# Feed-forward stages of a decoder trunk: two matmuls per weight tile instead of three, with the PSUM halves added at eviction

## What is computed

```python
D_MODEL, SEQ, DEPTH, D_FF = 1024, 256, 2, 2816
def swiglu(x, w_gate, w_up, w_down):
    return (jax.nn.silu(x @ w_gate) * (x @ w_up)) @ w_down
for i in range(DEPTH):
    h = h + 0.5 * swiglu(rms_norm(h, norm_ff1[i]), ffn1_gate[i], ffn1_up[i], ffn1_down[i])
    h = h + mixer_i(rms_norm(h, norm_mix[i]))
    h = h + 0.5 * swiglu(rms_norm(h, norm_ff2[i]), ffn2_gate[i], ffn2_up[i], ffn2_down[i])
return rms_norm(h, final_norm)
```

## Time and profile before

| | |
|---|---|
| median of 3 runs | 1134.71 us (1133.36 to 1139.84) |
| span of the profiled execution | 1132.6 us |
| PE busy | 1096.6 us, 97% |
| DVE busy | 752.8 us |
| ACT busy | 661.7 us |
| POOL busy | 169.1 us |
| mean DMA rate | 165 GB/s |

### The profile page before, as it was taken

How to read it: one execution, slowest core, us unless ns; L and a number is a source line. 1 busy time by engine, 2 the same in 40 slices (tenths; PEclk the granted TensorE clock), 3 DMA queues, 4 the chain that set the end, 5 groups by cost and what they waited for, 6 DMA issues and landing times.

```text
span 1132.6 us, 23053 instructions
## 1 busy us (share of the span) xinstructions
PE 1096.6 (97%) x8831; PEld 1068.1 (94%) x8831; DVE 752.8 (66%) x1028; ACT 661.7 (58%) x903; POOL 169.1 (15%) x156
## 2 busy tenths in 40 slices
PE   6999999999998999999999999999999989999996
PEld 5999999998888999999999999999988889999996
DVE  6666655799889766666546666654687677666643
ACT  5767643665876557675436676543545657676442
POOL 7000011223352420000120000012110040000011
PEclk9999999998999999999999999999999999999998
DMA  8766676444442656666765666765543336666761
GB/s 239 206 180 182 193 205 169 137 132 131 124 117 77 196 163 200 185 184 180 204 174 165 179 180 181 203 192 161 172 126 96 91 99 198 183 183 179 215 170 37
DMA packets 364307, 186.55 MB, mean 165 GB/s; under 512 B 5456, under 2 KB 363984, under 8 KB 364256
## 3 DMA queue, kind: packets, MB, share of 16 engines
q1 hardware_dynamic: 364000, 185.26, 57.7%
q0 software_dynamic: 256, 0.59, 0.2%
HBM read 184.78 MB, written 1.05 MB: 164 GB/s over the span
## 4 chain that ended last, share of the span: by engine, by line
PE 88%; DVE 7%; issue 2%; ACT 1%; POOL 1%; DMA 0%; DVEq 0%; ACTq 0%; SPq 0%; POOLq 0%
PE psum L187 27%; PE psum L188 27%; PE psum L189 27%; DVE wlo L175 1%; PE psum L1220 1%; DVE arena L868 1%; PE psum L1205 1%; POOL sumsq L270 1%; PE psum L639 1%; DVE xn L254 0%; PE psum L1219 0%; POOL sq L266 0%; DMA h<-in_xT 0%; PE psum L663 0%; DVE arena L856 0%
## 5 line engine op out<-in xcount | busy, mean ns | idle before, releaser
L187 PE MATMUL psum<-xn,whi 128*128 128x256 f32 x1888 | 543.6, 288 | 12.8 <-DVE wlo L175 12.2
L188 PE MATMUL psum<-xn,whi 128*128 128x256 f32 x1888 | 536.9, 284 | 0.0
L189 PE MATMUL psum<-xn,wlo 128*128 128x256 f32 x1888 | 536.6, 284 | 0.0
L175 DVE TENSOR_TENSOR wlo<-raw,whi 128x1024 fp32r<-128x1024 f32 (+1 forms) x317 | 419.2, 1341 | 42.4 <-ACT whi L170 41.6
L170 ACT ACTIVATE whi<-raw 128x1024 fp32r<-128x1024 f32 (+1 forms) x322 | 353.2, 1113 | 58.6 <-PE psum L189 53.2
L187 PEld LDWEIGHTS psum<-xn,whi 128*128 128x128 f32 x1888 | 364.6, 193 | 18.7 <-DVE wlo L175 10.5
L188 PEld LDWEIGHTS psum<-xn,whi 128*128 128x128 f32 x1888 | 365.2, 193 | 1.6 <-issue 1.4
L189 PEld LDWEIGHTS psum<-xn,wlo 128*128 128x128 f32 x1888 | 365.0, 193 | 0.0
L187 PE MATMUL psum<-hid,whi 128*128 128x256 f32 x896 | 254.2, 284 | 2.5 <-DVE hid L1011 1.6
L188 PE MATMUL psum<-hid,whi 128*128 128x256 f32 x896 | 253.5, 283 | 0.0
L189 PE MATMUL psum<-hid,wlo 128*128 128x256 f32 x896 | 253.5, 283 | 0.0
(11 more groups left out here) (186 smaller groups left out, 760.0 us busy)
## 6 DMA issues: line engine op xcount, KB each, us to landing
raw<-in_ffn_gate SPq DMA_DIRECT2D x88, 512.0 KB, 3.7
raw<-in_ffn_up SPq DMA_DIRECT2D x88, 512.0 KB, 4.8
raw<-in_ffn_down SPq DMA_DIRECT2D x64, 704.0 KB, 5.7
raw<-in_hyb_w_in SPq DMA_DIRECT2D x36, 512.0 KB, 3.7
raw<-in_dif_w_qkv SPq DMA_DIRECT2D x24, 512.0 KB, 4.3
raw<-in_hyb_w_out SPq DMA_DIRECT2D x16, 512.0 KB, 4.7
raw<-in_dif_w_o SPq DMA_DIRECT2D x8, 512.0 KB, 4.5
h<-in_xT SPq DMA_DIRECT2D x2, 512.0 KB, 5.4
```

The source lines that it names most:

```text
L175: dve.tensor_tensor(wlo[:, s, 0:k * P], raw[:, s, 0:k * P], whi[:, s, 0:k * P].bitcast(F32), ALU.subtract).then_inc(s_wlo, 1)
L187: pe.matmul(acc, w_hi, x[:, t, 0, :], start=start and j == 0, stop=False)
L188: pe.matmul(acc, w_hi, x[:, t, 1, :], start=False, stop=False)
L189: mm = pe.matmul(acc, w_lo, x[:, t, 0, :], start=False, stop=stop and j == k - 1)
```

## The change

For each weight tile one matmul of 512 columns multiplies `whi` with both parts of the activations, into a whole PSUM bank: the left half collects whi times the rounded part, the right half whi times the rest. A second matmul of 256 columns adds wlo times the rounded part to the right half. So a tile takes two matmuls, and a gate/up pair takes two banks; four banks hold two pairs. The output is the sum of the halves. For gate and up, ACT copies the right halves of both banks to the SBUF tile `cor` (`corrections`), DVE adds the left halves to it (`merge`, after which the banks are free), and a new DVE operation multiplies by `rb` (`normalize`). In the DVE step, the split of the gate block now stands ahead of the eviction, and the split of the up block between `normalize` and `product`. On ACT the copy stands between the two splits, and the silu behind the second. For the down products `down_out` adds the halves to `h` one after the other. The two mixers are as before.

```diff
+        def multiply_wide(pe, b, s, k, x, k0, acc, start=True, stop=True, need=None):
+            pe.wait_ge(s_wlo, b + 1)
+            for j in range(k):
...
+                pe.matmul(acc, w_hi, x[:, t, :, :], start=start and j == 0, stop=False)
+                mm = pe.matmul(acc[:, T:2 * T], w_lo, x[:, t, 0, :], start=False, stop=stop and j == k - 1)
+            mm.then_inc(s_blk, 1)
+        def wide(g, m):
+            return banks[(2 + m, m)[g]]
+        def wide_parts(g):
+            pair = psum[:, 2:4, :] if g == 0 else psum[:, 0:2, :]
+            return pair[:, :, 0:T], pair[:, :, T:2 * T]
...
+            def corrections(p, g):
+                act.wait_ge(s_blk, p * 2 + 2)
+                act.activation(cor[:, g, :, :], wide_parts(g)[1], ACT.Copy).then_inc(s_cor, 1)
...
-                act.wait_ge(s_gu, q + 1)
+                act.wait_ge(s_gn, q + 1)
                 act.activation(act_g[:, g, :], gu[:, g, 0, :], ACT.Silu).then_inc(s_silu, 1)
...
                         if m == 0:
-                            silu(it * 2 + (hb - 2 + g), g)
+                            corrections(it * 2 + (p0 - 2 + g), g)
+                    silu(it * 2 + (hb - 2 + g), g)
                     hidden_hi(it * 2 + (hb - 2 + g), g, it * 2 + (g - 2))
...
-            def scale(p, q, g, early=False):
+            def merge(p, q, g, early=False):
                 dve.wait_ge(s_blk, p * 2 + 2)
                 if not early:
                     dve.wait_ge(s_hlo, q - 1)
-                dve.tensor_tensor(gu[:, g, :, :], both(g), rb2, ALU.mult).then_inc(s_gu, 1)
+                dve.wait_ge(s_cor, q + 1)
+                dve.tensor_tensor(gu[:, g, :, :], wide_parts(g)[0], cor[:, g, :, :], ALU.add).then_inc(s_gu, 1)
+            def normalize(q, g):
+                dve.wait_ge(s_gu, q + 1)
+                dve.tensor_tensor(gu[:, g, :, :], gu[:, g, :, :], rb2, ALU.mult).then_inc(s_gn, 1)
...
-                scale(it * 2 + (p0 - 2 + g), q, g, early)
                 split_lo(dve, it * 4 + (2 * p0 + 2 * g), 2 * g, DT)
+                merge(it * 2 + (p0 - 2 + g), q, g, early)
+                normalize(q, g)
+                split_lo(dve, it * 4 + (2 * p0 + 2 * g + 1), 2 * g + 1, DT)
                 product(q, g)
-                split_lo(dve, it * 4 + (2 * p0 + 2 * g + 1), 2 * g + 1, DT)
                 hidden_lo(q, g, it * 2 + (g - 2))
...
-            add_residual(dve, n, d, half(p, 0), 0.5)
+            acc = wide(0, d % 2)
+            dve.scalar_tensor_tensor(h[:, d, :], acc[:, T:2 * T], 0.5, h[:, d, :], ALU.mult, ALU.add).then_inc(s_hr, 1)
+            dve.wait_ge(s_hr, hidden_before(n) // FT * DT + d + 1)
+            dve.scalar_tensor_tensor(h[:, d, :], acc[:, 0:T], 0.5, h[:, d, :], ALU.mult, ALU.add).then_inc(s_h, 1)
```

More of the change, by code:

```diff
@@ L127, in trunk @@
         s_gu = sem("s_gu")
+        s_cor = sem("s_cor")
+        s_gn = sem("s_gn")
         s_silu = sem("s_silu")
@@ L191, in multiply @@
                 mm.then_inc(s_blk, 1)
+        def multiply_wide(pe, b, s, k, x, k0, acc, start=True, stop=True, need=None):
+            pe.wait_ge(s_wlo, b + 1)
+            for j in range(k):
+                t = k0 + j
+                if need:
+                    need(t)
+                w_hi, w_lo = tile_of(whi, s, k)[:, j, :], tile_of(wlo, s, k)[:, j, :]
+                pe.matmul(acc, w_hi, x[:, t, :, :], start=start and j == 0, stop=False)
[6 more added lines that the diff above has]
+            return pair[:, :, 0:T], pair[:, :, T:2 * T]
         def half(pair, m):
@@ L270, in residual_square, with sums_bank @@
             pool.tensor_tensor(sumsq[:], sumsq[:], sq[:], ALU.add).then_inc(s_acc, 1)
+        def sums_bank(n):
+            wide_phase = n == len(phases) or phases[n][0] == "ffn"
+            return banks[4 if wide_phase else 2][:, 0:T]
         def token_sums(pe, n):
@@ L279, in token_sums @@
                 pe.wait_ge(s_const, 32)
-            mm = pe.matmul(SUMS, ones, sumsq[:], start=True, stop=not end)
+            mm = pe.matmul(sums_bank(n), ones, sumsq[:], start=True, stop=not end)
             if end:
                 pe.wait_ge(s_sq, (DT - 1) * (n + 1))
-                mm = pe.matmul(SUMS, ones, sq[:], start=False, stop=True)
+                mm = pe.matmul(sums_bank(n), ones, sq[:], start=False, stop=True)
             mm.then_inc(s_stat, 1)
@@ L289, in token_rms @@
                 act.wait_ge(s_rb, n)
-            act.activation(rms[:], SUMS, ACT.Sqrt, scale=1.0 / D, bias=eps[:, 0:1]).then_inc(s_rms, 1)
+            act.activation(rms[:], sums_bank(n), ACT.Sqrt, scale=1.0 / D, bias=eps[:, 0:1]).then_inc(s_rms, 1)
         def token_scale(dve, n):
@@ L332, in ffn_tensor, with gate_up @@
             p0, p1, hb = first[n], first[n] + FT, hidden_before(n)
-            def gate_up(p, g, need=None):
+            def gate_up(p, g, need=None, before_up=lambda: None):
                 for m in range(2):
-                    multiply(pe, p * 2 + m, 2 * g + m, DT, xn, 0, half(g, m), need=need if m == 0 else None)
+                    if m == 1:
+                        before_up()
+                    multiply_wide(pe, p * 2 + m, 2 * g + m, DT, xn, 0, wide(g, m), need=need if m == 0 else None)
             def down(p, g, need=None):
                 for m in range(2):
-                    multiply(pe, p * 2 + m, 2 * g + m, KD, hid, m * KD, half(g, 0), start=m == 0, stop=m == 1,
-                             need=need)
+                    multiply_wide(pe, p * 2 + m, 2 * g + m, KD, hid, m * KD, wide(0, g), start=m == 0, stop=m == 1,
+                                  need=need)
             if n:
                 read_out(pe, p0 - 2)
-            gate_up(p0, 0, lambda t: pe.wait_ge(s_xlo, DT * n + t + 1))
+            gate_up(p0, 0, lambda t: pe.wait_ge(s_xlo, DT * n + t + 1), lambda: read_out(pe, p0 - 1))
             token_sums(pe, n)
-            if n:
-                read_out(pe, p0 - 1)
             gate_up(p0 + 1, 1)
@@ L451, in ffn_vector @@
                     q = hb + FT - 2 + e
-                    scale(p0 + FT - 2 + e, q, e)
+                    merge(p0 + FT - 2 + e, q, e)
+                    normalize(q, e)
                     product(q, e)
```

8 lines of the change are left out of this document (5 added, 3 removed).

## The result

The changed kernel takes 1186.28 us (median of 4 runs, 1185.86 to 1186.99) against 1134.28 us before in the same series: ratio 1.0443, 95% interval 1.042 to 1.0466, slower. (The ratio is taken over all runs of both kernels, so it can differ by up to 0.2% from the quotient of the medians, here 1.0458.) The span is 1184.8 us, 52.2 us longer.

The account below looks back on a forecast made before the run. PE (97% busy) bounded the kernel before; a DVE/ACT cycle would bound the changed gate/up loop. Four stages +45.2, kernel end +0.5, clock +6.5: 1134.7 + 52.2 = 1187 us; range 1180 to 1194 from the clock, 1171 to 1206 overall.

Parts of the forecast that it names:

- The ring: Gate/up loop: DVE and ACT rows wait on each other in a cycle, 5.76 us odd step, 7.21 even; PE waits.
- rival b: Gate/up loop: cycle shorter, PE bounds, 1084 us; with one table load off the chain 1135 or 1129; chance 0.06.
- Its length: Gate/up loop: an iteration of DVE and ACT takes 12.97 us, PE needs 10.75; before it was 11.52.
- The tile: PE: 0.216 us for 512 columns and 0.120 for 256, so 0.336 us a weight tile against 0.360 before.
- rival (a): PE: tile of 0.347 or 0.360 us, down half longer by 1.9 or 4.2 us a stage: 1195 or 1204; chance 0.13.
- the surplus of 0.013 us: PE at full clock: 256 columns take 0.120 us, not 0.107; put to a step beside the stream, such as the next weight load.
- Rival (d): PE: 512 columns cost hardly more than 0.120 us, tile 0.240 us, kernel 1119 us; chance 0.02.
- A whole stage: Feed-forward stage: 201.8 against 190.5 us, +11.3; +15.5 up to the first down matmul, -4.2 in the down half.
- The border and the clock: Start of the down half: PE waits 4 us, then 3.4 us at half clock lose 1.6; +6.5 in four stages.
- rival (c): Gate/up loop: clock falls again and again, PE bounds there at mixed clock, 1210 us and more; chance 0.07.
- Small terms: Down evictions: second addition to `h` hidden between stages, +0.5 us at the kernel's end; DMA loads costed at nothing.

Follow-up runs that it names:

- Experiment 1: Changed kernel with the loop's rows on DVE and ACT back in the order before the change: 1122.65 us, ratio 0.9866.
- 5: Changed kernel plus one unused 128x512 DVE operation as last row of the loop's odd step: 1186.8 us, ratio 1.0463.
- experiment 6: Changed kernel plus one unused 128x512 DVE operation between normalize and the second split in the loop's odd step: 1209.11 us, ratio 1.0654.
- experiment 2: Changed kernel with the silu replaced by a plain copy, so the loop has no table loads: 1130.62 us, ratio 0.9935.
- experiment 8: Kernel before plus eight series of 32 unused matmuls, one form each, single run: pitch 0.120 us for 256 fp32r columns (128 weight columns), 0.227 for 512.
- experiment 7: Changed kernel plus twelve unused 512-column matmuls ahead of the first down block in each feed-forward stage: 1177.8 us, ratio 1.0375.
- experiment 4: Kernel before with only the new order of the loop's rows on DVE and ACT: 1137.33 us, ratio 1.0004.

## Why the prediction was right, step by step

**The ring.** Right: it sets the loop's period. Experiment 1 shows that order is the cause; 5 and 6 that a place in the ring is what costs; 2 that the table load lies in it (rival b's mechanism, which does turn the sign: 1130.62 us where 1129 to 1135 was reckoned). Wrong is where PE was to wait, in each pair by 1.8 and 0.4 us in turn. It waits once per iteration, 1.0 us on average: the short step takes 5.55 us where 5.76 was forecast, the pair on PE 5.65 where 5.38 was, so nothing is left to wait for.

**Its length.** 12.97 us forecast, 12.52 measured, less than the 12.9 to 13.0 that was to show it. Two handovers were taken from a timeline in which ACT, by its rows, was waiting for PE's blocks: the turn of the loop (0.24) and hidden_hi to split (0.08). When the block is long done, the table load follows hidden_hi directly (71.74 + 0.42 = 72.16, load at 72.17) and the next split even overlaps it by 0.1. That is 0.4 of the 0.45 us by which an iteration is shorter, and the 0.45 make 18 us in 40.

**The tile.** The term that was undersized: 0.336 us forecast for the tile, 0.347 to 0.353 measured. The down halves of the changed kernel all ran at 0.353. That is the sign named for rival (a), and its mechanism did occur: 8 x 22 x 0.017 = 3.0 us in the down half of each stage, 12 in all. The step that failed is the reading of the earlier trace rows, where plain f32 matmuls come 0.217 us apart, as the price of 512 fp32r columns. It is 0.227 alone and 0.23 to 0.24 in the kernel. With it fails the argument that the surplus of 0.013 us over a tick per column does not belong to the columns: by experiment 8 some 0.007 us of it do, at full clock, and 0.006 go with the weight columns. The faster tile, 0.347, is the sum of the two pitches measured alone; what adds 0.006 us in the slower one stays open. Rival (d), 512 columns at hardly more than 0.120 us, is out by the same 0.227.

**A whole stage.** The second feed-forward stage runs from 422.14 to 560.78 to its first down matmul, 138.6 us where 142.7 was forecast, and from there to the next stage's first matmul at 624.56 another 63.8, where 59.1 + 1.6 was. The sum is 202.4, 11.9 over the 190.5 of before; forecast was 11.3 + 1.6. The third takes 139.3 + 65.0 = 204.3 us, since half clock lasted longer there. The shorter ring (18 us too much in the sum) and the longer tile (12 us too little) mostly cancel. So the mechanism was right, but that the forecast of 1187 us lies within 1 us of 1186.28 is luck.

**The border and the clock.** PE waited 3.1 to 3.5 us, 4 forecast, and half clock followed each time, as it did after 2.53 and 1.84 us in the earlier trace rows. Forecast were 3.4 us at half clock and a loss of 1.6 us at each border, 6.5 in all. At three borders it was 3.4 us and 1.5, at the third 6.1 us and 2.8, some 7.3 in all; experiment 7 removes it. Where half clock lasted 3.4 us, the first down matmuls still ran at full clock for 1.0 to 1.4 us. In the loop's gaps of 1.2 us the clock stayed at full, so rival (c) did not occur. It was nearer than that sounds: its gaps were reckoned at 1.8 us, and in experiment 6, where they are that long, the clock did fall in the loop. The length of the wait alone does not decide: 1.77 us was followed by half clock there, 2.30 us in experiment 2 was not. What does was not tested.

**Small terms.** The attention stage was 1.5 us longer in the changed kernel's trace (141.55 against 140.07). There PE waits 2.07 us for L1525, as it did before (2.06), but this time 3.4 us at half clock follow, which would cost about 1.7 if every matmul in them took twice as long. Why the clock fell this time was not tested.

## What to carry to other kernels

An engine with time to spare is no reserve if its next row stands behind a wait. Before rows are moved, follow each engine's order and the semaphores between them around a closed loop, add it up once, and compare it with the bound's period: here the order of the rows cost 64 us once a normalize had been added to the ring, and nothing without it (experiment 4). The whole change, with a quarter of all matmuls taken out, won 14 us once the old order stood again. Where a pipelined loop splits operands and evicts results on the same engines, try the eviction first and the product between the splits. At the loop's border the same took away PE's wait of 1 us a stage.

## What was not expected of the hardware

At full clock 256 columns, of bf16 or of fp32r with 64 weight columns, take 0.114 us and 512 of fp32r 0.227, so 0.44 ns a column, 6 to 7% over a tick of 2.4 GHz. At half clock fp32r columns take one tick of 1.2 GHz (0.213 us for 256). With 128 weight columns, 256 fp32r columns take 0.120 us, and 128 columns still 0.110. A stream of alternating 512- and 256-column matmuls without a wait settles into one of two paces for half a stage, 0.353 or 0.347 us a tile, at the same granted clock and the same work.
